# Index items of a sparse-attention layer sent to the array in pairs instead of one by one

## The reference

```
s     = einsum('bqhd,bsd->bqhs', q_idx, k_idx)        # 16 heads of 64
score = einsum('bqhs,bqh->bqs', relu(s), w_idx)       # weighted sum over the heads
score = where(causal, score, -inf);  _, idx = top_k(score, 128)
logits = q . k[idx];  o = softmax(logits) @ v[idx]    # per block of 128 queries
```

## Time and profile before

| | |
|---|---|
| median of three executions | 2506.09 us |
| the profiled execution, its own time | 2506.65 us |
| its span, first to last instruction | 2504.8 us |
| instructions | 26889 |
| PE busy, share of the span | 2410.6 us, 96% |
| DVE busy | 1007.8 us, 40% |
| POOL busy | 973.4 us, 39% |
| ACT busy | 626.1 us, 25% |
| mean granted TensorE clock | 0.979 |

### The profile page before, as it was taken

One profiled execution on the slowest core, in us unless ns is written; L12 is line 12 of the kernel. 1 busy time (PEld: TensorE's weight loads), 2 busy tenths in 40 slices (PEclk: granted clock), 3 DMA queues, 4 the chain that ended last, 5 costly groups with the idle time before them and its releaser, 6 DMA issues.

```text
span 2504.8 us, 26889 instructions
## 1 busy us (share of the span) xinstructions
PE 2410.6 (96%) x10926; PEld 1942.5 (78%) x10926; DVE 1007.8 (40%) x1430; ACT 626.1 (25%) x822; POOL 973.4 (39%) x414
## 2 busy tenths in 40 slices
PE   6999978899999899989999999999999999999999
PEld 3687557688877687878888888888888888888887
DVE  2225799866766476763122122122031131221221
ACT  4222321222222222232222122122222222221221
POOL 1332233234433333434444444444444444444442
PEclk8989999899999899999999999999999999999999
DMA  9954345557754742223222332322333322223331
GB/s 379 348 200 151 118 151 185 185 178 257 247 176 167 251 135 85 76 86 108 78 91 101 101 100 100 95 91 82 100 100 100 100 100 80 89 99 101 101 118 51
DMA packets 183650, 342.16 MB, mean 137 GB/s; under 512 B 4337, under 2 KB 31124, under 8 KB 182804
## 3 DMA queue, kind: packets, MB, share of 16 engines
q1 hardware_dynamic: 174944, 336.77, 39.4%
q10 hardware_dynamic: 8628, 4.28, 0.6%
HBM read 324.26 MB, written 16.78 MB: 136 GB/s over the span
## 4 chain that ended last, share of the span: by engine, by line
PE 84%; DVE 10%; DMA 4%; issue 1%; ACT 1%; SPq 0%; POOL 0%; ACTq 0%; DVEq 0%
PE pj L1160 48%; PE pa L1160 30%; DVE part_rows L974 3%; DMA ada_first<-w_ada_in 2%; PE pa L1345 1%; DMA ada_rows<-w_ada_in 1%; DVE score L890 1%; PE pa L1227 1%; DVE m L889 1%; PE pa L1164 1%; DVE sq L1136 1%; DMA resid<-xT_dram 1%; PE pa L1379 1%; DMA rows<-vecs 0%; PE pa L1221 0%
## 5 line engine op out<-in xcount | busy, mean ns | idle before, releaser
L692 POOL TENSOR_TENSOR w_lo<-raw,w_hi 128x1024 fp32r<-128x1024 f32 (+1 forms) x396 | 954.4, 2411 | 1465.0 <-ACT w_hi L486 1464.9
L486 ACT ACTIVATE w_hi<-raw 128x1024 fp32r<-128x1024 f32 (+1 forms) x396 | 417.1, 1054 | 1628.0 <-PE pj L1160 1054.5
L1160 PE MATMUL pj<-h,w_hi 128*128 128x512 f32 x1664 | 523.3, 396 | 4.2 <-DVE h L785 2.5
L1160 PE MATMUL pj<-w_hi,h 128*128 128x512 f32 (+1 forms) x1536 | 484.2, 391 | 8.8 <-DVE rot L930 8.8
L1160 PEld LDWEIGHTS pj<-h,w_hi 128*128 128x128 f32 x1664 | 312.6, 190 | 81.2 <-issue 17.1
L1136 DVE TENSOR_TENSOR sq<-relu 128x512 f32<-128x512 f32 x64 | 160.5, 2508 | 515.6 <-ACT relu L648 515.6
L1160 PE MATMUL pa<-h,w_hi 128*128 128x512 f32 x1152 | 358.8, 393 | 0.0
L1160 PEld LDWEIGHTS pj<-w_hi,h 128*128 128x128 f32 x1536 | 289.0, 192 | 86.6 <-issue 17.5
L1160 PE MATMUL pj<-h,w_lo 128*128 128x512 f32 x832 | 326.5, 392 | 0.0
L1160 PE MATMUL pj<-mid,w_hi 128*128 128x512 f32 x1024 | 317.8, 392 | 5.6 <-DVE mid L1140 5.6
L1160 PE MATMUL pa<-mid,w_hi 128*128 128x512 f32 x1024 | 316.2, 390 | 0.0
(11 more groups left out here) (160 smaller groups left out, 1526.7 us busy)
## 6 DMA issues: line engine op xcount, KB each, us to landing
raw<-w_mlp_in SPq DMA_DIRECT2D x64, 2048.0 KB, 8.8
ada_rows<-w_ada_in SPq DMA_DIRECT2D x64, 1024.0 KB, 5.1
raw<-w_in_in SPq DMA_DIRECT2D x22, 2048.0 KB, 8.3
ada_first<-w_ada_in SPq DMA_DIRECT2D x32, 1024.0 KB, 11.7
raw<-w_out_in SPq DMA_DIRECT2D x8, 2048.0 KB, 8.5
ret<-ret_dram SPq DMA_DIRECT2D x32, 256.0 KB, 4.0
raw<-w_in_in SPq DMA_DIRECT2D x4, 1792.0 KB, 14.4
x_nat<-x_in SPq DMA_DIRECT2D x4, 1024.0 KB, 10.1
```

The source lines that it names most:

```text
L486: act.activation(split_chunk(w_hi, u, j), raw_chunk(u, j), ACT.Copy).then_inc(hi_done, 1)
L692: pool.tensor_tensor(split_chunk(w_lo, u, j), raw_chunk(u, j), split_chunk(w_hi, u, j).bitcast(F32), ALU.subtract).then_inc(lo_done, 1)
L1160: last = pe.matmul(dst, lhs[a], rhs[b], start=start and n == 0, stop=stop and n == 2)
```

## The change

In a token chunk the four items no longer go out as one after `tb` = 0, one after `tb` = 1 and two after `tb` = 2, but as two after `tb` = 0 and two after `tb` = 2. In a feature chunk the six items no longer go out singly after `kk` = 1 to 6, but as two after `kk` = 1, two after `kk` = 3 and two after `kk` = 6. The wait for a free bank is made once for the two, ahead of the even one, for the value that the odd one needs. The lists of ACT, DVE, POOL and SP are as they were.

```
@@ -1179,8 +1179,9 @@
                     if tb == NB - 1:
                         last.then_inc(chunk_used, 1)
-                    for n in items[slice(*((0, 1), (1, 2), (2, 4), (4, 4))[tb])]:
-                        index_item(n)
+                    if tb % 2 == 0:
+                        for n in items[tb:tb + 2]:
+                            index_item(n)
@@ -1193,8 +1194,10 @@
                     if kk == 7:
                         last.then_inc(chunk_used, 1)
-                    for n in items[kk - 1:kk] if kk else ():
-                        index_item(n)
+                    if kk in (1, 3, 6):
+                        first = 2 * (1, 3, 6).index(kk)
+                        for n in items[first:first + 2]:
+                            index_item(n)
@@ -1340,7 +1343,8 @@
                 if n % 4 == 3:
                     pe.wait_ge(mod_taken, done["mods"])
-                need(pe, idx_taken, n - 3)
+                if n % 2 == 0:
+                    need(pe, idx_taken, n - 2)
                 pe.wait_ge(iq_ready, 4 if n < 24 else 8)
```

## The result

The changed kernel takes 2489.89 us (median of four executions, 2487.38 to 2492.37), the kernel before 2506.06 us (four executions with the three shown ahead); the ratio is 0.9937, 95% interval 0.9922 to 0.9952. The prediction was 2489.0 us, range 2486.6 to 2493.6.

A forecast was written before the change was run, and what follows sets the result against it. PE was taken to bound the kernel from 228 to 341 us, DVE right behind; gains of 2.3 + 10.5 + 4.3 = 17.1 us gave 2489.0 us, range 2486.6 to 2493.6 us.

The forecast's parts named there:

- The price of one and of a pair: On PE, an item costs 0.84, 1.06 or 1.26 us by width, a pair's second nothing; 18 groups fewer, 19.0 us.
- Rival C: Pairs in feature chunks save only a fixed 0.42 us per group: gain 11.0 us, 2495.1 us; chance 0.07.
- The end of chunk 24: Three groups fewer save 2.5 us; PE's modulation sum waiting for ACT's ReLUs takes back 0.2: gain 2.3 us.
- Chunks 25 to 29: Fewer groups save 10.1 + 1.7 us; ACT's late query-tile copy at chunk 28 takes back 1.3: gain 10.5 us.
- Chunks 30 to 35: PE loses 4.6 us, but DVE has only 4.3 us of waiting to give and becomes the bound: gain 4.3 us.
- Rival B: DVE arrives late at `square_q`, its 4.3 us of room eaten by long accumulations: gain 12.8 us, 2493.3 us; chance 0.13.
- Rival D: PE waits at the pairs for a bank, behind ACT and DVE, some 3 us per chunk: slower, 2513 us; chance 0.02.
- Rival E: The stretch behind 341 us is set by something other than `square_q` and eats the gain: 2506 us; chance 0.02.

The follow-up runs named there:

- fours: Changed kernel with items sent four then two in feature chunks and all four together in token chunks: 2483.24 us, ratio 0.9923 to the kernel before.
- the fours with the early copy: Changed kernel with groups of four in all chunks and ACT's query-tile copy ahead of the weight split: 2482.31 us, ratio 0.9911 to the kernel before.

## Why the prediction was right

**The price of one and of a pair.** Right. Prices of 0.84, 1.06 and 1.26 us, six groups each, gave 19.0 us; a pair in a feature chunk costs 0.02 to 0.03 us more than one item. Rival C (a pair saves only the fixed part) is what the kernel with both items in one half does, at 2501.5 us: it takes two items on the same rows to make it true.

**The end of chunk 24.** Predicted 2.3 us. From the first item to DVE's pick-up it was 10.03 us (229.02 to 239.05), now 7.82 (228.48 to 236.30): 2.2.

**Chunks 25 to 29.** Predicted 10.5 us. 53.88 us became 43.15: 10.7. The copy made PE wait 1.16 us where I had 1.6, and DVE waited for `stage` in chunks 25 to 27, all told,

```profile
DVE score L879 <- ACT stage L559: 1.3, 3, 0.9
```

where I had worked out 2 of the 10.3 us of the earlier trace rows. DVE's last addition of chunk 27 ends 28.7 us after the pick-up, as forecast, but by luck: it waited 0.7 us less and worked 0.6 us longer than reckoned. Nor are PE and DVE equal there. The chain that ended last runs through DVE and ACT from 244.50 us until the copy lets PE go, with `stage` and `part_rows` between these rows:

```profile
244.50 0.63 DVE score L879
...
264.84 0.60 ACT iqT L521
265.44 0.14 issue
265.57 0.70 PE pa L1349 x4
```

The order of events was as followed there; ACT's timeline at the end of chunk 27 answers to the earlier trace rows:

```profile
263.40 0.60 ACT L559 ACTIVATE stage<-pa 128x512 f32<-128x512 f32 x1 [0.26 <-DVE score L879]
263.89 1.05 ACT L486 ACTIVATE w_hi<-raw 128x1024 fp32r<-128x1024 f32 x1
264.84 0.59 ACT L521 ACTIVATE iqT<-pj 128x512 f32<-128x512 f32 x1
```

The last ReLU has changed its releaser, from PE to DVE.

**Chunks 30 to 35.** Predicted 4.3 us, got 48.43 - 43.89 = 4.54. The reason given for 4.3 rather than 4.6, that DVE would be the bound, was wrong. DVE still waited 0.4 us for items and 0.84 us for `nat`; its work was 43.89 - 1.28 = 42.6 us, not 44.1. I had taken its work as a constant, but the accumulations are longer where POOL's split of a weight chunk runs beside them. DVE's timeline, answering to the row of 304.20 us in the earlier trace rows:

```profile
289.64 3.95 DVE L974 SCALAR_TENSOR_TENSOR part_rows<-ada_rows,csilu,part_rows 128x512 f32<-128x512 f32 x4
298.17 3.58 DVE L974 SCALAR_TENSOR_TENSOR part_rows<-ada_rows,csilu,part_rows 128x512 f32<-128x512 f32 x4
306.86 3.44 DVE L974 SCALAR_TENSOR_TENSOR part_rows<-ada_rows,csilu,part_rows 128x512 f32<-128x512 f32 x4
```

of which the kernel before had the next two as

```profile
312.71 4.08 DVE L974 SCALAR_TENSOR_TENSOR part_rows<-ada_rows,csilu,part_rows 128x512 f32<-128x512 f32 x4
...
322.17 3.88 DVE L974 SCALAR_TENSOR_TENSOR part_rows<-ada_rows,csilu,part_rows 128x512 f32<-128x512 f32 x4
```

and POOL's splits in the stretch of the changed kernel:

```profile
288.30 2.38 POOL L692 TENSOR_TENSOR w_lo<-raw,w_hi 128x1024 fp32r<-128x1024 f32 x1 [6.02 <-ACT w_hi L486]
296.44 2.39 POOL L692 TENSOR_TENSOR w_lo<-raw,w_hi 128x1024 fp32r<-128x1024 f32 x1 [5.76 <-ACT w_hi L486]
304.98 2.41 POOL L692 TENSOR_TENSOR w_lo<-raw,w_hi 128x1024 fp32r<-128x1024 f32 x1 [6.14 <-ACT w_hi L486]
```

The split ends at 290.68, 298.83 and 307.39 us, that is 1.04, 0.66 and 0.53 us into the accumulation, which takes 3.95, 3.58 and 3.44. The kernel before has 1.03, 1.16 and 0.98 us of overlap with 3.94, 4.08 and 3.88. The less they overlap, the shorter it is, in all six nearly one for one. The three are 0.9 us shorter in sum, the piece of a modulation row ahead of `square_q` another 0.8 (4.04 us instead of 4.84). That this is the cause was read from the traces and not tested by itself. So 4.3 us came out nearly right by luck: two errors, DVE's work and DVE as the bound, met. Rival B, DVE late at `square_q`, did not happen, with pairs nor with fours.

**Rival D, PE held at the pairs.** No matmul of the changed kernel waits for `stage`; two weight loads name it, with the same 0.35 us of idle time as those of the other pairs. Such a wait of a matmul appears without pairs (0.67 us) and in the fours with the early copy (0.88 us), both times not at an item but at the modulation sum of chunk 29, which waits for all items.

The rule that I weighed for B (the Trainium skill, TensorEngine Tiling (Array Packing), PSUM Bottleneck: the emptying of PSUM may become the bottleneck) holds as a direction. It is seen in the copy for which PE waits 1.16 us, in 17.5 gained; with the split out of its way 0.54 us of wait are left. In the feature chunks, with groups of four, it grows by 0.8 us, half of what they save.

**Rival E.** Wrong: all 17.5 us arrive, within the 2163 to 2167 us that the rest takes by chance. The span of the profiled execution shows 16.3 of them, and the medians 16.2.

## What to carry to other kernels

Matmuls that use half of the rows should stand in pairs of opposite halves with nothing between them: here the second was free, and each group between full-array matmuls had a fixed price on top, 0.42 us. Take that price from starts, not durations, and multiply it by groups, not by instructions. Then follow the chain behind the shared bank item by item: what limited this packing next was one copy that stands in an engine's list behind work which the late engine holds up, and not how fast PSUM is emptied on the average. And where two profiles differ by a stretch at the lower clock, take that out before you judge the order of the work.

## What the runs showed of the hardware

- One PE wait of 1.98 us, with PE busy until then, was followed by some 3 us at the lower of the two clock levels (granted clock 0.55 over 3.3 us), which cost 1.56 us: in that execution the wait cost nearly twice its length. After waits of 1.16 us at the same place, in three profiles, the clock stayed at 1.00. More than one profile would be needed to say that the longer wait brings it down each time.
- Two items of 256 columns cost 1.28 us in one half of the array (225.64 to 228.28 us, less six projections), two in both halves 0.85 (228.48 to 230.69 us); four of 512, two in each half, save 0.46 us against two pairs.
- Four accumulations of 128x512 on DVE took 3.44 to 4.08 us in chunks 30 to 33, with a split of POOL beside them for the first 0.53 to 1.16 us, and 5.1 to 5.3 us with all of one beside them.
- From one execution to the next the first item starts anywhere from 223.7 to 229.0 us, and the rest of the kernel behind `square_q` takes 2162.6 to 2166.6 us, while the 112 us between them repeat to 0.01 us. A stretch between two fixed events of the traces tells steps of 0.1 us apart where medians of five executions need some 3, as long as the clock is the same in both.
